# Reciprocal roots of two norms computed as a power on GpSimd instead of a square root on ScalarE and a reciprocal on VectorE

## The reference

```python
def rms_norm(x, g):
    y = x * lax.rsqrt(jnp.mean(x * x, axis=-1, keepdims=True) + EPS)
    return y * g

u = rms_norm(h, norm_mix_g)
a, g, q, k, v = split(u @ w_in)                  # five parts of 512
conv_out = silu(layer_norm(conv(a * sigmoid(g)) + conv_b))
# differential attention: 4 heads of value width 128, blocks of 128 queries
o = pd @ v                                        # pd = softmax_0 - lam * softmax_1
attn_out = rms_norm(o, subln_g) * (1 - lambda_init)      # the head norm, over 128 values
h = h + concat(conv_out, attn_out) @ w_out
hn = rms_norm(h, norm_ffn_g)                      # the residual norm, over 1024 values
h = h + moe_ffn(hn, ...)                          # 32 experts, the best 4 of each token
```

## Time and profile before

| | us |
|---|---|
| median of 3 runs | 1508.72 |
| lowest and highest | 1507.97, 1511.87 |
| the profiled execution | 1509.68 |
| its span, first to last instruction | 1508.1 |
| TensorE busy in the span | 1427.4 (95%) |
| VectorE busy | 1281.3 (85%) |
| ScalarE busy | 1000.1 (66%) |
| GpSimd busy | 257.0 (17%) |

### The profile page before, as it was taken

How to read it: one execution, slowest core, us unless ns; L and a number is a source line. 1 busy time by engine, 2 the same in 40 slices (tenths; PEclk the granted TensorE clock), 3 DMA queues, 4 the chain that set the end, 5 groups by cost and what they waited for, 6 DMA issues and landing times.

```text
span 1508.1 us, 19819 instructions
## 1 busy us (share of the span) xinstructions
PE 1427.4 (95%) x6444; PEld 1161.3 (77%) x6444; DVE 1281.3 (85%) x1030; ACT 1000.1 (66%) x943; POOL 257.0 (17%) x279
## 2 busy tenths in 40 slices
PE   7996799939999999999999999999999999999996
PEld 5885447836788888888888888888888888888884
DVE  3499865555899999999999999999999999999994
ACT  5344264424677777777777777777777777777773
POOL 2000000150011122111221111121122111221111
PEclk9998679958999999999999999999999999999998
DMA  9220002657799999999999999999999999999971
GB/s 314 99 88 25 1 1 76 233 102 298 275 378 374 382 375 370 365 359 373 381 364 376 374 355 373 372 360 367 385 354 388 361 353 375 378 370 368 369 279 20
DMA packets 94695, 445.18 MB, mean 295 GB/s; under 512 B 14863, under 2 KB 14879, under 8 KB 61840
## 3 DMA queue, kind: packets, MB, share of 16 engines
q1 hardware_dynamic: 80704, 421.82, 73.7%
q0 software_dynamic: 11392, 17.61, 4.9%
q10 hardware_dynamic: 2576, 5.46, 1.4%
HBM read 439.43 MB, written 22.43 MB: 306 GB/s over the span
## 4 chain that ended last, share of the span: by engine, by line
PE 87%; DVE 9%; DMA 1%; ACT 1%; issue 1%; POOL 0%; ACTq 0%; POOLq 0%
PE psum L1170 25%; PE psum L1172 25%; PE psum L1171 25%; DVE acc L867 5%; PE psum L1418 2%; PE psum L1443 2%; PE psum L1427 2%; PE psum L1242 1%; DVE wlo L822 1%; DMA slot_table<-payload,dest 1%; PE psum L1452 1%; PE psum L1302 1%; PE psum L1360 1%; PE psum L1177 0%; PE psum L1244 0%
## 5 line engine op out<-in xcount | busy, mean ns | idle before, releaser
L1076 DVE TENSOR_TENSOR wlo<-ring,whi 128x2048 fp32r<-128x2048 f32 x384 | 871.8, 2290 | 88.6 <-ACT whi L724 84.8
L724 ACT ACTIVATE whi<-ring 128x2048 fp32r<-128x2048 f32 x384 | 736.9, 1919 | 244.0 <-PE psum L1172 244.0
L1170 PE MATMUL psum<-whi,xT_hi 128*128 128x512 f32 x1024 | 403.2, 394 | 2.8 <-DVE xT_lo L1082 2.8
L1171 PE MATMUL psum<-whi,xT_lo 128*128 128x512 f32 x1024 | 400.2, 391 | 0.0
L1172 PE MATMUL psum<-wlo,xT_hi 128*128 128x512 f32 x1024 | 400.1, 391 | 0.0
L1170 PEld LDWEIGHTS psum<-whi,xT_hi 128*128 128x128 f32 x1024 | 193.4, 189 | 42.8 <-DVE xT_lo L1082 3.6
L1172 PEld LDWEIGHTS psum<-wlo,xT_hi 128*128 128x128 f32 x1024 | 193.2, 189 | 40.4
L1171 PEld LDWEIGHTS psum<-whi,xT_lo 128*128 128x128 f32 x1024 | 193.5, 189 | 39.1
L1170 PE MATMUL psum<-whi,aT_hi 128*128 128x512 f32 x512 | 203.1, 397 | 1.9 <-ACT y_sb L747 1.9
L1172 PE MATMUL psum<-wlo,aT_hi 128*128 128x512 f32 x512 | 200.4, 392 | 0.0
L1171 PE MATMUL psum<-whi,aT_lo 128*128 128x512 f32 x512 | 199.7, 390 | 0.0
(11 more groups left out here) (236 smaller groups left out, 1378.4 us busy)
## 6 DMA issues: line engine op xcount, KB each, us to landing
ring<-in_w_gate_up SPq DMA_DIRECT2D x256, 1024.0 KB, 7.5
ring<-in_w_down SPq DMA_DIRECT2D x128, 1024.0 KB, 6.7
ring<-in_w_in SPq DMA_DIRECT2D x10, 1024.0 KB, 13.9
ring<-in_w_out SPq DMA_DIRECT2D x4, 1024.0 KB, 5.1
h<-in_x SPq DMA_DIRECT2D x4, 512.0 KB, 5.4
hn_rows<-hn ACTq DMA_DIRECT2D x4, 512.0 KB
out<-h ACTq DMA_DIRECT2D x4, 512.0 KB, 2.6
bias_rows<-rows_st SPq DMA_DIRECT2D x1, 1280.0 KB, 14.9
```

The source lines that it names most:

```text
L724: nc.scalar.activation(whi[:, hi_of(number), :], ring[:, slot(number), :], ACT.Copy).then_inc(hi_ready, 1)
L1076: TT(wlo[:, slot(number), :], ring[:, slot(number), :], whi[:, hi_of(number), :].bitcast(F32), ALU.subtract).then_inc(lo_ready, 1)
L1170: MM(o, s_hi, m_hi, start=first, stop=False)
L1171: MM(o, s_lo, m_hi, start=False, stop=False)
```

## The change

The two norms' reciprocal roots are computed on GpSimd, as (sum / count + EPS) to the power -0.5, in two instructions: a multiply and add, and a power with a column that holds -0.5. The head norm's runs once over 16 columns, the residual norm's four times over one column. On ScalarE the square roots L666 and L680 and the root of a constant, L705, are gone; on VectorE the reciprocals L963 and L991. GpSimd makes one more constant at the start. The new instructions stand in GpSimd's queue behind the iota of L431, ahead of its wait for the front's last weight chunk and of the six index tables.

```diff
@@ @block.gpsimd: constants
             const(nc.gpsimd.memset(eps, EPS))
+            const(nc.gpsimd.memset(minus_half, -0.5))
@@ @block.gpsimd: behind the iota of payload
+            def power(dst, src, count, squares, done):
+                nc.gpsimd.tensor_scalar(dst, src, 1.0 / count, EPS, ALU.mult, ALU.add).then_inc(root_step, 1)
+                pool.wait_ge(root_step, squares)
+                nc.gpsimd.tensor_tensor(dst, dst, minus_half.to_broadcast([P, dst.shape[1]]), ALU.pow).then_inc(done, 1)
+
+            pool.wait_ge(o_evac, T * (H + 1))
+            power(rstdo[:, :], so[:, :], DV, 1, o_std)
+            for t in range(T):
+                pool.wait_ge(act_step, T + t + 1)
+                power(rstd2[:, t:t + 1], ss2[:, t:t + 1], D, t + 2, ss2_done)
 
             pool.wait_ge(chunk_used, N_FRONT)
@@ @block.scalar
             o_out(T - 1)
-            act.wait_ge(o_evac, T * (H + 1))
-            nc.scalar.activation(rstdo[:, :], so[:, :], ACT.Sqrt, bias=eps, scale=1.0 / DV).then_inc(o_std, 1)
@@ root(t)
                 nc.scalar.activation(hn[:, t, :], h1[:, t, :], ACT.Square, accum_out=ss2[:, t:t + 1]).then_inc(act_step, 1)
-                act.wait_ge(act_step, T + t + 1)
-                nc.scalar.activation(rstd2[:, t:t + 1], ss2[:, t:t + 1], ACT.Sqrt, bias=eps, scale=1.0 / D).then_inc(ss2_done, 1)
@@ behind gates_exp(0)
-            nc.scalar.activation(spare, eps, ACT.Sqrt)
@@ @block.vector
             dve.wait_ge(o_std, 1)
-            link(nc.vector.reciprocal(rstdo[:, :], rstdo[:, :]))
             link(TS(rstdo[:, :], rstdo[:, :], 1.0 - LAMBDA_INIT, None, ALU.mult))
@@ normalise(t)
-                link(nc.vector.reciprocal(rstd2[:, t:t + 1], rstd2[:, t:t + 1]))
                 STT(out=hn[:, t, :], in0=h1[:, t, :], scalar=rstd2[:, t:t + 1], in1=g_ffn[:, :],
```

More of the change, by code:

```diff
@@ L111, in build @@
         qg, kg, sg = vecs[:, 20:21], vecs[:, 21:22], vecs[:, 22:23]
-        eps, spare = vecs[:, 23:24], vecs[:, 29:30]
+        eps, minus_half = vecs[:, 23:24], vecs[:, 29:30]
         lam2, rlam = vecs[:, 24:26], vecs[:, 26:28]
@@ L242, in build @@
         out_done, h1_done, payload_made = sem("out_done"), sem("h1_done"), sem("payload_made")
+        root_step = sem("root_step")
         ss2_done, hn_ready, hnT_done, hnT_evac, logits_done = (
```

## The result

The changed kernel takes 1512.31 us in the median of 20 executions (1509.94 to 1516.13), the kernel before 1509.95 in 20 executions beside it (1507.16 to 1512.09). The ratio is 1.0017, with a 95% interval from 1.0010 to 1.0024: slower by some 2.5 us, which is less than 0.3%. The forecast was 1508.8 with a range from 1505 to 1514, and no measurable difference.

What follows compares the result with a forecast made beforehand. TensorE, busy 1427.4 of 1508.1 us, bounds the kernel; the change only moves when the items begin. Head norm 0, tile 3 +0.12, the rest 0 make +0.1 us; from the runs' median, 1508.8 us, range 1505 to 1514.

Steps and rivals of the forecast that it cites:

- The sum itself: Whole change on the profiled execution: head norm 0, tile 3's residual norm +0.12, removed work 0; +0.1 us, 1509.68 to 1509.8.
- Where the path lies: Front: TensorE not waiting at the head norm, residual norm hidden for tiles 0 to 2, tile 3 delaying everything one for one.
- The cover of 0.43 us: Head norm: VectorE's seventh-part `add_tile` ends at 262.73, TensorE wants it at 263.16, so 0.43 us of lateness is free.
- The rule max(0, p16 - 1.95): Head norm's cost in us: what p16 takes beyond 1.95; forecast as nothing.
- p16: Head norm: duration of GpSimd's power over 16 columns, forecast at 1.46 us.
- The hops and the multiply and add: Around each power: three engine hops of 0.08 us and a GpSimd multiply and add of 0.18, together 0.42 us.
- The power itself: GpSimd's power in both norms: 0.18 us plus 0.08 a column, the middle ratio between 0.006 and 0.98.
- p1: Residual norm: duration of GpSimd's power over one column, forecast at 0.26 us; tile 3 costs p1 - 0.14.
- rival A: Power dear per column, mainly at the head norm: up to +18 us, 1527; chance 0.17 for 0.11-0.37 us a column, 0.13 above.
- the signs for the forecast: 16-column power ends before 259.5, TensorE without gap 258.6 to 291.5, tile 3's `hn` 0.6-0.8 us after squares, four fewer table loads.
- rival B: Head norm: the program's first power pays a code-loading delay, 0 to 3.05 us, up to +2.7 us, 1511.5; chance 0.09.
- What goes away beside it: Four ScalarE table loads go, GpSimd's later queue catches up before the third scatter group, added constant is hidden: 0 us.

Runs made afterwards that it cites:

- the four parts: Changed kernel with the head norm's power taken in four instructions of four columns, each once its block of queries is done: 1509.96 us, ratio 1.0014 to the kernel before.
- the last kernel: Changed kernel with 16 more GpSimd instructions (powers, then products, 1 to 32 columns) behind the last scatter; ran once, its time not used.

## Why the prediction was right or wrong

*The number.* The measured median lies 3.5 us above the forecast and inside the range. About 1.2 us of that is no fault of the reasoning on the change: the forecast stood on the median of three executions, 1508.72, and the median of twenty is 1509.95. Of the rest 1.4 us is the power, which was mis-sized, and about 1 us is open. The sum itself (+0.1 us) was off by 1.3 us. That the forecast of no difference beyond 0.3% held is due to the reading of the path, and to luck: the price of a column was the middle of a bracket from 0.006 to 0.98 us, and it happened to lie within a factor of two.

*Where the path lies*: right. TensorE alone at the head norm with some cover, tile 3's residual norm bare, tiles 0 to 2 covered (19.85 to 19.90 us between A and B in every kernel).

*The cover of 0.43 us*: right. The head norm's scale came 3.36 - 1.94 = 1.42 us later and A grew by 1.02 to 1.06 us, so 0.36 to 0.40 were covered. The rule max(0, p16 - 1.95) gives 1.00 for the measured 2.95 us. That an earlier scale is worth nothing was shown by the four parts: 0.54 us earlier, A unchanged.

*The hops and the multiply and add*: right. 0.42 us was assumed around the power, 3.36 - 2.95 = 0.41 measured.

*The power itself* is the term that was mis-sized. I took 0.08 us a column on 0.18; it is 0.157 on 0.38. That made p16 1.46 where it is 2.95, and p1 0.26 where it is 0.54. The head norm went from nothing to +1.02 and tile 3 from +0.12 to +0.38: together +1.4 instead of +0.1 us. The fixed part failed because a copy's 0.18 us was taken for it; a product of two operands has that price too (0.19), so the other 0.2 us comes with the power. The case that came was the mild end of rival A, between 0.11 and 0.37 us a column, which had been priced at 1509.5 to 1513. (By the prediction's own rule the lower end is 1508.9: at 0.11 us a column the head norm costs nothing and tile 3 costs 0.15.) Its sign had been named: TensorE stands for 0.56 us ahead of the transposes of `o_tok`, at 266.07. Of the signs for the forecast two failed with it, the early end of the power and `hn` at 0.6 to 0.8 us after the squares (0.93).

*The first power* (rival B): not so. The first of the program took 1.06 us over four columns and the second took 1.02; in the one profile where the first took longer, 1.44 us, it had begun beside a VectorE instruction. Neither excess is near the 3.05 us allowed for.

*What goes away beside it*: right. Four table loads fewer (14 before, 10 after), the gates' 1.10 us spent in the next wait, GpSimd caught up before the third group. The trace's 1.28 us a load was the right price.

*The last microsecond.* The median moved by 2.4 us and the stages account for 1.4. The first pair of profiles seems to supply the rest in C, but C is not a property of the kernel: with the last scatter at the same place behind `hn` to 0.07 us, it was 46.03 and 44.20 in two profiles of the kernel before, 47.03 and 43.74 in two of the changed one, and 42.53 to 45.39 in the other kernels without a new wait. One kernel in two sets of executions moved from +0.94 to -0.92. The changed kernel with its constant elsewhere was at +0.6. The three kernels that were set against the last 29 executions of the kernel before all came out under their stages (the changed one and the one in four parts, both with the late constant, by 0.8 and 0.2 us, the constant alone by 0.9), where the earlier ones with a power or the constant came out over theirs; so the microsecond seems to go with the set of executions and not with the kernel. The profiles can't settle one microsecond elsewhere either: the sixth `add_tile` begins between 257.5 and 262.5 us in them, in kernels with the change and without, and from the first item's first matmul to the end of the span it is 1164.7 to 1167.6 us (the last kernel with its added instructions aside). So 1.4 us is shown, and whether anything else is the change's is open; the first set's interval, 1.5 to 3.6 us, only just excludes 1.4 by itself.

## What to carry to other kernels

Take a function's price on a software engine from a measurement for each column, not from that engine's cheap operations: a product of 16 columns cost 0.21 us and a power 2.9. Work out the cover of a step to the tenth of a microsecond before moving it, since the cost is what lies beyond it, one for one; and if most of the columns are ready earlier, take the function in parts and leave only the last ones on the path. Where two profiles differ in a DMA's landing, read a second profile of each kernel before calling it a cause.

## What the runs showed of the hardware

- The power of GpSimd's two-operand instruction takes 0.38 us + 0.157 us a column of 128 values, from 1 to 32 columns (0.54 us for one, 5.41 for 32). The first one of a program, over four columns, took 1.06 us where later ones took 1.01 to 1.02, and 1.44 us in a profile where a VectorE instruction still ran beside its start.
- A semaphore count in GpSimd's program that stands behind an indirect DMA came before the DMA's instruction began (VectorE, waiting for it, started 0.09 us ahead of the last scatter, and 0.17 us ahead of the gather at the second count). It doesn't mark the end of the instruction ahead of it.
- From the start of the last of 16 scatters to the next GpSimd instruction that waits for all of them it took 7.9 to 12.3 us, with the last scatter at the same place behind `hn` to 0.07 us, and 11.3 us with VectorE silent for the last 5.8 of them.
